# Mask by matmul, late normalisation, and the recurrent branch as one block ahead of the attention units

## The reference, cut to what matters

```python
q, k, v, qi, ki, wi, xr, yg = jnp.split(h @ w_in[l], split_at, axis=-1)   # q, k, qi, ki rotated
attn_out = dsa_attention(q, k, v, qi, ki, wi)      # 4 heads of 128; an indexer picks 128 causal keys a query
xc = causal_depthwise_conv(xr, conv_w[l], conv_b[l])
# rg_lru: r, i = sigmoid(block-diagonal gates of xc); log_a = -8 * r * softplus(-lam); a = exp(log_a)
#   u = sqrt(-expm1(2 * log_a)) * (i * xc);  h_t = a_t * h_(t-1) + u_t along the 512 tokens
lru_out = rg_lru(xc, ...) * jax.nn.gelu(yg, approximate=True)
merged = jnp.concatenate([rms_norm(attn_out, g_attn_out[l]), rms_norm(lru_out, g_lru_out[l])], axis=-1)
mix = merged @ w_out[l]
x = layer_norm(alpha * x + (1.0 + g1) * mix, ln1_g[l], ln1_b[l])
```

## Time and profile before

| | |
|---|---|
| median of 3 runs | 1457.12 us (1449.92 to 1457.58) |
| profiled execution, its own time | 1457.48 us |
| its span, first to last instruction | 1455.8 us |
| granted TensorE clock, mean | 0.941 |
| TensorE matmul busy | 1328.1 us (91%) |
| VectorE busy | 868.3 us (60%) |
| ScalarE busy | 561.0 us (39%) |
| GpSimd busy | 85.4 us (6%) |

### The profile page before, as it was taken

The page is one execution under the profiler, slowest core; times in us unless marked ns, Lnnn a source line. Parts: engine busy times, 40 slices in busy tenths (PEclk is TensorE's granted clock), DMA queues, the critical chain, the costliest instruction groups (busy, mean ns, idle before and its releaser), DMA issues.

```text
span 1455.8 us, 17039 instructions
## 1 busy us (share of the span) xinstructions
PE 1328.1 (91%) x6152; PEld 1042.6 (72%) x6152; DVE 868.3 (60%) x1502; ACT 561.0 (39%) x853; POOL 85.4 (6%) x95
## 2 busy tenths in 40 slices
PE   4799979479999999999999997957999999999997
PEld 4677656267788888888877774624778888888886
DVE  6765579965674453735567457997475443343454
ACT  1663425452462332423347342545246333142231
POOL 2000000000100000000030000000020000000012
PEclk9799989689899999999999998968899999999998
DMA  8653424211134234243244433520113333323321
GB/s 273 205 174 126 144 87 159 92 40 44 57 103 159 86 102 157 86 158 102 87 119 158 145 116 106 171 85 1 44 44 117 94 94 101 96 91 101 101 73 59
DMA packets 73399, 158.58 MB, mean 109 GB/s; under 512 B 6528, under 2 KB 10872, under 8 KB 73336
## 3 DMA queue, kind: packets, MB, share of 16 engines
q1 hardware_dynamic: 60480, 110.70, 24.4%
q0 software_dynamic: 12224, 46.66, 9.6%
q10 hardware_dynamic: 632, 0.39, 0.1%
HBM read 155.64 MB, written 2.10 MB: 108 GB/s over the span
## 4 chain that ended last, share of the span: by engine, by line
PE 78%; DVE 17%; DMA 2%; issue 2%; ACT 1%; ACTq 0%; SPq 0%; POOL 0%; POOLq 0%; DVEq 0%
PE bank L587 23%; PE bank L589 22%; PE bank L588 22%; DVE idx_acc L1482 4%; DVE best L1480 3%; DVE w_lo L1299 2%; PE bank L615 2%; DMA x_in<-in_x_dram 2%; PE bank L494 1%; PE bank L552 1%; PE bank L808 1%; PE bank L667 1%; DVE lru_gate L1527 1%; DVE small L1554 1%; DVE turned_ring L1433 1%
## 5 line engine op out<-in xcount | busy, mean ns | idle before, releaser
L1299 DVE TENSOR_TENSOR w_lo<-w_raw,w_hi 128x1024 fp32r<-128x1024 f32 (+1 forms) x216 | 237.0, 1112 | 356.9 <-ACT w_hi L890 356.7
L587 PE MATMUL bank<-a_hi,w_hi 128*128 128x512 f32 x896 | 372.4, 416 | 18.6 <-issue 11.5
L890 ACT ACTIVATE w_hi<-w_raw 128x1024 fp32r<-128x1024 f32 (+1 forms) x216 | 202.7, 959 | 473.7 <-PE bank L589 473.5
L588 PE MATMUL bank<-a_lo,w_hi 128*128 128x512 f32 x896 | 353.4, 394 | 0.0
L589 PE MATMUL bank<-a_hi,w_lo 128*128 128x512 f32 x896 | 353.2, 394 | 0.0
L587 PE MATMUL bank<-b_hi,w_hi 128*128 128x512 f32 x640 | 249.9, 390 | 1.2 <-issue 1.2
L589 PE MATMUL bank<-b_hi,w_lo 128*128 128x512 f32 x640 | 249.1, 389 | 0.0
L588 PE MATMUL bank<-b_lo,w_hi 128*128 128x512 f32 x640 | 249.0, 389 | 0.0
L587 PEld LDWEIGHTS bank<-a_hi,w_hi 128*128 128x128 f32 x896 | 171.0, 191 | 73.6 <-issue 32.9
L588 PEld LDWEIGHTS bank<-a_lo,w_hi 128*128 128x128 f32 x896 | 171.2, 191 | 39.6 <-issue 4.1
L589 PEld LDWEIGHTS bank<-a_hi,w_lo 128*128 128x128 f32 x896 | 170.7, 191 | 36.9
(11 more groups left out here) (254 smaller groups left out, 1365.9 us busy)
## 6 DMA issues: line engine op xcount, KB each, us to landing
mod_raw<-in_w_mod_dram POOLq DMA_DIRECT2D x40, 1024.0 KB, 5.9
w_raw<-in_w_up_dram SPq DMA_DIRECT2D x64, 512.0 KB, 3.7
w_raw<-in_w_down_dram SPq DMA_DIRECT2D x64, 512.0 KB, 3.7
w_raw<-in_w_in_dram SPq DMA_DIRECT2D x48, 512.0 KB, 3.7
w_raw<-in_w_out_dram SPq DMA_DIRECT2D x16, 512.0 KB, 6.2
first_mod<-in_w_mod_dram SPq DMA_DIRECT2D x4, 1024.0 KB, 22.4
first_mod<-in_w_mod_dram POOLq DMA_DIRECT2D x4, 1024.0 KB, 14.6
x_in<-in_x_dram SPq DMA_DIRECT2D x4, 512.0 KB, 23.2
```

The source lines that it names most:

```text
L587: mm(o, wh, hi[:, kk, :], start=first, stop=False)
L588: mm(o, wh, lo[:, kk, :], start=False, stop=False)
L890: last = af(hi, src, ACT.Copy)
L1299: last = tt(lo, src, hi.bitcast(F32), ALU.subtract)
```

## The change

The arithmetic that leads to the output is the same in exact numbers. What is done where changes as follows.

- **Mask.** VectorE writes the selection as a float32r tile of 0 and -2^100 (`mask_of`), and TensorE adds it to the scores with a float32r matmul with the identity as its weights. The scale 128 ** -0.5 is folded into q's copy out of PSUM. VectorE then only takes the negated row maximum from PSUM (`row_max`), and the exponential reads PSUM too. `masks` makes tile 0's mask in the slot of group k.
- **Normalisation.** The probabilities are transposed unnormalised. `values` yields tokens on the partitions, and `attn_tile` divides a whole tile of four heads by the sums in one instruction. Mean squares of the attention come from ScalarE's accumulator (`attn_squares`). `turn_tile` multiplies each token tile with a diagonal matrix of the reciprocal roots, which transposes and normalises it, in four places within group out0.
- **Recurrent branch.** It stands as one block: `decays` straight after the gates, all `lru_input`, the last nine rounds of `topk`, all `lru_scan`, squares, `lru_sums` on TensorE, and the root. Then come the units. GpSimd squares `a` (`lru_a2`), which was VectorE's L1518. The split of the recurrent rows (`lru_merge`, `lru_high`, `lru_low`) lies between units 2 and 6, `spread` in unit 1.
- **Order at the end.** out0 can begin with the recurrent rows when the units are through.

```diff
+        lru_a2 = sb("lru_a_squared", [P, LT, T], F32, a_at + 12 * K2)
+        an = sb("attn_tokens", [P, TT, AW], F32, a_at + 12 * K2)
...
+                    if n == LATE_PAIRS - 2:
+                        for m in range(LT):
+                            pool.wait_ge(decay_done, l * LT + (m + 1))
+                            gp.tensor_tensor(lru_a2[:, m, :], lru_a[:, m, :], lru_a[:, m, :], ALU.mult).then_inc(lru_squared, 1)
...
+            def mix_ready(base):
+                def wait(kk, n):
+                    pe.wait_ge(b_lo_s, base + (n + 1 if n < LT else DK))
...
-                    mm(banks[b][:, 0:(i + 1) * P], q[:, h, i * P:(i + 1) * P], k[:, h, 0:(i + 1) * P],
-                       start=True, stop=True).then_inc(full_s[b], 1)
+                    o = banks[b][:, 0:(i + 1) * P]
+                    mm(o, q[:, h, i * P:(i + 1) * P], k[:, h, 0:(i + 1) * P], start=True, stop=False)
+                    pe.wait_ge(mask_ready, l * TT + (i + 1))
+                    mm(o, ident_r[:, :], mask_of(i), start=False, stop=True).then_inc(full_s[b], 1)
...
-                    pe.wait_ge(attn_p, l * 16 + (u + 1))
+                    pe.wait_ge(free_s[5 + u % 2], uses_before(5 + u % 2, f"s{u}", l) + 1)
...
-                        last = mm(banks[b][:, h * P:(h + 1) * P], v[:, j, h * DH:(h + 1) * DH],
-                                  probs_t[:, u % 2, j * P:(j + 1) * P], start=(j == 0), stop=(j == i))
+                        last = mm(banks[b][:, h * DH:(h + 1) * DH], probs_t[:, u % 2, j * P:(j + 1) * P],
+                                  v[:, j, h * DH:(h + 1) * DH], start=(j == 0), stop=(j == i))
...
+                def lru_sums():
+                    pe.wait_ge(sq_ready, l * LT + LT)
+                    pe.wait_ge(free_s[4], uses_before(4, "lms", l))
+                    for t in range(TT):
+                        for m in range(LT):
+                            last = mm(banks[4][:, t:t + 1], sq_l[:, m, t * P:(t + 1) * P], ones_d[:, 0:1],
+                                      start=(m == 0), stop=(m == LT - 1))
+                    last.then_inc(full_s[4], 1)
...
                 scores(0)
                 scores(1)
+                lru_sums()
...
+                    if u == 1:
+                        pe.wait_ge(diag_done, l * 3 + 1)
+                        spread(4, "lrb", l, diag_l)
                     turned(u)
                     if u >= 1:
                         values(u - 1)
                 values(len(UNITS) - 1)
...
+                def turn_tile(i):
+                    def run():
+                        b = 5 + i % 2
+                        pe.wait_ge(root_diag_s, l * TT + (i + 1))
+                        pe.wait_ge(free_s[b], uses_before(b, f"at{i}", l))
+                        for h in range(HEADS):
+                            last = mm(banks[b][:, h * P:(h + 1) * P], an[:, i, h * DH:(h + 1) * DH], root_diag[:, i % 2, :],
+                                      start=True, stop=True)
+                        last.then_inc(full_s[b], 1)
+                    return run
+                group("out0", l, mix_hi, mix_lo, mix_ready(l * (5 * DK)), order=OUT_ORDER, between={4: turn_tile(0), 6: turn_tile(1), 11: turn_tile(2), 13: turn_tile(3)})
...
+                for m in range(LT):
+                    act.wait_ge(free_s[4], uses_before(4, f"gr{m}", l) + 1)
+                    af(lru_a[:, m, :], th[:, m, :], ACT.Exp, scale=neg_sp[:, m:m + 1]).then_inc(decay_done, 1)
+                for m in range(LT):
+                    act.wait_ge(decay_done, l * LT + (m + 1))
+                    af(th[:, m, :], th[:, m, :], ACT.Tanh, scale=vcol("lru_lambda", m)).then_inc(lru_exp, 1)
                 def expo(u):
                     i, h = UNITS[u]
+                    b, n = 5 + u % 2, (i + 1) * P
                     act.wait_ge(attn_max, l * 16 + (u + 1))
-                    pr = probs[:, u % 4, 0:(i + 1) * P]
-                    af(pr, pr, ACT.Exp, bias=negm[:, u:u + 1], scale=SCALE, accum_out=rsum[:, u:u + 1]).then_inc(attn_exp, 1)
+                    if u >= 3:
+                        b3 = 2 + (u - 3) % 2
+                        act.wait_ge(full_s[b3], uses_before(b3, f"pt{u - 3}", l) + 1)
+                    af(probs[:, u % 3, 0:n], banks[b][:, 0:n], ACT.Exp, bias=negm[:, u:u + 1],
+                       accum_out=rsum[:, u:u + 1]).then_inc(free_s[b], 1)
...
-                def attn_tile_out(i):
+                def attn_squares(i):
                     b = i % 2
...
+                    act.wait_ge(free_s[b], uses_before(b, f"o{i}", l) + 1)
+                    af(ring[:, i, :], an[:, i, :], ACT.Square, accum_out=attn_ss[:, i:i + 1]).then_inc(attn_sq, 1)
+                def mix_roots(n, lo, hi):
+                    act.wait_ge(var_done, n)
+                    af(mix_var[:, lo:hi], mix_var[:, lo:hi], ACT.Sqrt).then_inc(root_done, 1)
...
+                def lru_high(m):
+                    act.wait_ge(m_full, l * LT + (m + 2))
+                    af(lru_hi[:, m, :], xc[:, m, :], ACT.Copy).then_inc(b_hi_s, 1)
+                for m in range(LT):
+                    act.wait_ge(lru_m, l * LT + (m + 1))
+                    af(th[:, m, :], th[:, m, :], ACT.Sqrt).then_inc(lru_sqrt, 1)
+                for m in range(LT):
+                    act.wait_ge(lru_out, l * LT + (m + 1))
+                    af(sq_l[:, m, :], xc[:, m, :], ACT.Square).then_inc(sq_ready, 1)
+                mix_roots(l * 5 + 1, 0, TT)
                 for u in range(len(UNITS)):
                     expo(u)
                     if u >= 1:
                         probs_turned(u - 1)
...
+                    if 2 <= u < 2 + LT:
+                        lru_high(u - 2)
+                    if u in (7, 11, 15):
+                        attn_squares(u // HEADS - 1)
                 probs_turned(len(UNITS) - 1)
...
+                mix_roots(l * 5 + 2, TT, 2 * TT - 1)
+                attn_squares(TT - 1)
+                mix_roots(l * 5 + 3, 2 * TT - 1, 2 * TT)
+                def attn_high(i):
+                    b = 5 + i % 2
+                    act.wait_ge(free_s[b], uses_before(b, f"at{i}", l) + 1)
+                    af(attn_hi[:, :, i * P:(i + 1) * P], by_head(at_full[:, i % 2, :]), ACT.Copy).then_inc(b_hi_s, 1)
+                for i in range(TT):
+                    attn_high(i)
                 act.wait_ge(mod_used, l * MOD_PAIRS + (NEXT_PAIRS + LATE_PAIRS))
                 af(mod_rows[:, :], banks[7][:, :], ACT.Copy).then_inc(mod_rows_s, 1)
...
+                def masks():
+                    ve.wait_ge(conv_done, l * LT + LT)
+                    step(v_.tensor_copy(ident_r[:, :], ident[:, :]))
+                    step.settle()
+                    ts(mask_0[:, :], causal[:, (TT - 1) * P:], -BIG, -MASKED, ALU.is_equal, ALU.mult).then_inc(mask_ready, 1)
...
+                    ve.wait_ge(lru_squared, l * LT + (m + 1))
+                    stt(th[:, m, :], lru_a2[:, m, :], 1.0, th[:, m, :], ALU.add, ALU.mult).then_inc(lru_m, 1)
...
-                def mask_scores(u):
+                def row_max(u):
                     i, h = UNITS[u]
                     b = 5 + u % 2
-                    n = (i + 1) * P
                     ve.wait_ge(full_s[b], uses_before(b, f"s{u}", l) + 1)
...
+                    v_.reduce_max(negm[:, u:u + 1], banks[b][:, 0:(i + 1) * P], AX_X, negate=True).then_inc(attn_max, 1)
+                def attn_tile(i):
+                    b, us = i % 2, slice(i * HEADS, (i + 1) * HEADS)
...
+                    tt(by_head(an[:, i, :]), by_head(banks[b][:, :]), rinv[:, us].unsqueeze(2).broadcast_to([P, HEADS, DH]),
+                       ALU.mult).then_inc(free_s[b], 1)
+                def mix_vars(n):
+                    if n == 1:
+                        ve.wait_ge(full_s[4], uses_before(4, "lms", l) + 1)
...
+                def mix_recips(n, lo, hi):
+                    ve.wait_ge(root_done, l * 5 + n)
+                    step(v_.reciprocal(mix_root[:, lo:hi], mix_var[:, lo:hi]))
                     step.settle()
...
+                def token_diag(i):
+                    if i >= 2:
+                        ve.wait_ge(full_s[5 + i % 2], uses_before(5 + i % 2, f"at{i - 2}", l) + 1)
+                    ts(root_diag[:, i % 2, :], ident[:, :], mix_root[:, TT + i:TT + i + 1], None, ALU.mult).then_inc(root_diag_s, 1)
+                def lru_merge(m):
+                    ve.wait_ge(full_s[4], uses_before(4, "lrb", l) + 1)
+                    stt(xc[:, m, :], xc[:, m, :], vcol("g_lru_out", m), banks[4][:, :], ALU.mult, ALU.mult).then_inc(m_full, 1)
+                def lru_low(m):
+                    ve.wait_ge(b_hi_s, l * (5 * DK) + (m + 1))
+                    tt(lru_lo[:, m, :], xc[:, m, :], lru_hi[:, m, :].bitcast(F32), ALU.subtract).then_inc(b_lo_s, 1)
+                def attn_merge(i):
+                    b = 5 + i % 2
+                    if i >= 2:
+                        ve.wait_ge(b_lo_s, l * (5 * DK) + (LT + i - 1))
```

(49 more changed lines are left out.)

236 lines of the change are left out of this document (82 added, 154 removed).

## The result

The changed kernel takes 1465.44 us (median of 15 runs, 1459.51 to 1468.73), the kernel before 1453.92 us (15 runs, 1448.92 to 1458.02). The ratio is 1.007, with a 95% interval of 1.0053 to 1.0086: slower by 0.7%. The profiled execution took 1465.05 us, its span 1463.3 at a mean granted clock of 0.942.

What follows compares the result with a forecast made beforehand. VectorE was taken to pace the stage's first part, TensorE the next, waits the tail. Units ending at 334.9 plus tail 4.2 gave 339.1 against 335.11: 4.0 us more a layer, 8 for two, about 1465 us, range 1450 to 1482.

Steps and rivals of the forecast that it cites:

- a ring: From unit 1: row maximum, exponential, ScalarE's copy, lru_high, lru_low, next row maximum; 2.6 us a unit, four turns 10.4.
- a tail without waits: out0 starts at once on the recurrent rows, where before it came 14.65 us after the last values.
- The recurrent block: Inputs, nine topk rounds and scans on VectorE from 255.96 to 287.2 us, TensorE having nothing to do: 31.3 us.
- The sums and the root: lru_sums at half clock, 6.96 us, then variance, root, table load and first exponential, to 297.3 us.
- Units 0 to 6: First attention units: 16.4 us at full clock, 20.3 at half, taken as 18.
- Units 7 to 15: Later attention units, TensorE setting the pace at full clock: 18.8 us together, mask matmul 0.23 at 512 columns.
- The 0.8 for weight loads: Allowance per layer, in us, for mask matmul weight loads that short matmuls don't hide.
- The tail: out0 carries four turn_tiles of 0.92, 3.7 in all, plus small waits: costs 4.2 us.
- the stall that I put at 0.3: In out0, TensorE arrives at 14.6 us, the second half's low parts end at 14.9: 0.3 us.
- B: Rival: clock back at once, sums in 3.6 us, units 0 to 6 in 16.4; 1455 us, chance 0.18.
- C: Rival: ring of units 2 to 6 doesn't close, units 0 to 6 take 9 us; 1440 or 1447, chance 0.11.
- D: Rival: half clock well into the dense units; 1486 us if to unit 11, 1508 for all, chance 0.18.

Runs made afterwards that it cites:

- the fifth experiment: The changed kernel with lru_merge, lru_high and lru_low moved from units 2 to 6 to units 8 to 12: 1458.62 us, ratio 1.0031.
- the square of four: Layer 0 stage lengths: kernel before 103.2 us, the same with branch in front 107.7; rebuilt attention with branch between the units 88.1, with branch in front 107.3.
- the first experiment: The changed kernel with the recurrent branch threaded between the rebuilt attention's units again: 1428.51 us, ratio 0.9805.

## Why the prediction was right, and where it was not

The forecast was 1465 us, 8 over before, as the sum of one lost overlap, slow sums and a ring, less a tail without waits. That the total came out to the microsecond is partly luck. It was built on the 1457.12 of three runs, and fifteen runs have a median of 1453.92; 8 over that is 1462. The loss of 8 agrees with the profiled pair, 7.5, and the medians lie 11.5 apart. Point by point, in layer 0:

- **The recurrent block** (31.3 forecast; 255.95 to 288.73, 32.8). The rounds took 14.0 (264.32 to 278.30) and the scans 2.59 each, as priced. The inputs took 8.4 and not 6.9. This is the term that was sized worst: I took GpSimd's effect on VectorE as nothing with 0.9 as the upper end, from adds at 823 ns. Seven instructions from 258.41 at the 0.605 that undisturbed ones take from start to start end at 262.65; they ended at 264.32. So it cost 1.7 us, and lay outside my bounds. The row that gave them was a mean of two kinds: of the 24 adds, sixteen took 0.69 and eight 1.00 to 1.18, which the 823 hides. The Trainium skill (GPSIMD Engine Reference, section 1, Specifications) names instructions with two SBUF inputs as those that contend; the runs agree, up to 1.53 for these and 0.69 for MAX8. My estimate from that page, up to 2 us over both layers, was nearer than the nothing that I took, and still short of 2 x 1.7.
- **The sums and the root** (6.96 forecast, 6.98 measured; the first exponential forecast for 297.3). All of the 1.5 us was handed on, the first exponential ending at 298.8.
- **Units 0 to 6** (18 forecast, 17.5 measured: 298.85 to 316.36). The size is right, its parts less so. I interpolated between a full clock and a half one. The clock was 0.50 up to 307 us, that is through unit 0, `spread` and two turns of the ring, and about 1 from there. The ring turned in 2.10, 2.10, 2.88 and 2.45 us from maximum to maximum, against 2.6 forecast for each. The turns of 2.10 are the same at either clock; the one with the `late_mod` is not. With the split moved away, in the fifth experiment, the same units took 11.8 (297.05 to 308.86).
- **Units 7 to 15** (18.8 + 0.8 forecast, 18.4 measured: 316.36 to 334.73). The mask matmul cost 0.23 as priced: with 512 keys, scores and mask took 1.10 (322.39 to 323.49), 0.86 without. The 0.8 for weight loads that show wasn't needed. That and the 0.5 in units 0 to 6 paid back the block's 1.5, so that out0 began at 334.73, forecast 334.9.
- **The tail** (+4.2 forecast). From out0's first matmul to `turn_mods` it took 26.6 (334.73 to 361.37), before 21.9 (335.11 to 356.97): +4.8. The four `turn_tile`s are 1.05 long, but 0.81 from start to start, 3.2 together and not 3.7, and the stall that I put at 0.3 was 0.28. Most of the other 1.3 is single matmuls of out0 that start later than 0.23 after the one before, as at its first use of bank 1 (335.28 to 335.76) and behind each turn (338.75 to 339.06). The sum had only the 0.2 of bank 1 for this; it is a term that was put too low.

The stage was to be 4.0 us longer and is, by 4.1 in layer 0 and 3.5 in layer 1, with errors of +1.5 in the block, -1.7 in the units and +0.6 in the tail that nearly cancel, by luck. So the predicted total holds better than its terms.

Of the rivals, B (1455, the clock comes back at once) fails on both halves: from 289 to 296 us TensorE is busy 6.55 of 7 us at a granted clock of 0.50, and from 298.85 to 307 it is again 0.50. The Trainium skill (TensorE: Matmul & The Clock Gate, Part 1) says that activity releases the throttle; here an engine that is busy by the profile with one-column matmuls stays at the lower level, and the measurement decides. C (1440 to 1447, the ring doesn't close) fails because in the changed kernel the ring did close. The late split comes near to it, 11.8 for units 0 to 6 against C's 9, with a clock of 0.82 in them and not the full one that C had; the stage gained 3.1 only, since the split must be done somewhere. D (1486 or more) fails on the window from 313.6 at a clock of 1.00.

What the change did as a whole is shown by the square of four: the rebuilding, with the recurrent tail that it moves, is worth 15 us a layer, and all of it is lost again when the block stands in front. More than half of that loss comes back with the block where it is, once its waits are filled.

## What to carry to other kernels

An order of work is only as good as what lies beside it: ahead of moving a VectorE block out of a TensorE stretch, add up what TensorE did under it (here 12.4 us in 25) and what its return at half clock costs. Price short splits that alternate between two in-order engines as a ring, in which each turn adds to the main loop, and put the parts of a reduction behind the parts that feed it. When filling a wait leaves the time unchanged, look at what now stands first in the same engine's order, as here the variance in front of the row maxima. And a mean over a group of instructions may mix two kinds: ask for the shortest and the longest before pricing by it.

## What was not expected of the hardware

GpSimd and VectorE slow each other only with some instructions: MAX8 and MATCH_REPLACE8 beside GpSimd's squares kept their 1.51 us a round, while two-input fp32 instructions of 128x512 went from 0.69 to 1.53 us and squares from 1.03 to 1.5. Both kinds read 128x512 fp32 from SBUF. And they seem to take turns rather than to share. In the rows of GpSimd and VectorE above, each long instruction ended a fixed time after the other engine's instruction that had begun before it: VectorE's two some 0.55 us after a square's end (260.55 after 260.00, 261.99 after 261.44), GpSimd's three some 0.90 after the end of VectorE's instruction (257.53 after 256.64, 260.00 after 259.10, 261.44 after 260.55). The other layer and the first experiment show the same. The 1.36 that I had read as GpSimd's price is again a mean of two kinds, adds of 1.28 and of 1.44 to 1.56:

```profile
L473 POOL TENSOR_TENSOR ln_q<-ln_q,ln_sq x24: 1280/1288/1560, 361.5 to 1437.9; 128x512 f32<-128x512 f32 x24
L1394 DVE TENSOR_TENSOR ln_s<-ln_s,resid x24: 691/693/1178, 360.7 to 1437.2; 128x512 f32<-128x512 f32 x24
```

These are views of the two lines in the kernel before, with the shortest, median and longest in ns. Why a square alone takes 1.03 and an add 1.28, no run shows.

Sixteen one-column float32 matmuls (32 pieces) took 6.98 us behind an idle TensorE and 3.65 behind a busy one, though the profile calls TensorE busy in both. In the second case the clock fell to 0.50 all the same, just as they ended. And the stage of kernels that are the same up to it begins up to 5 us earlier or later in one execution than in another, of which I can say only that it arises ahead of the stage.
